# Spreading the expert gates in one pass instead of two, with half of them parked in HBM and part of the one-hot work on ScalarE

## The chip, the core and the metric

One core of a Trainium2 chip runs the whole kernel in one launch. The metric is the device time in microseconds, lower is better. Engines: TensorE (PE, with its weight loads as PEld), VectorE (DVE), ScalarE (ACT), GpSimd (POOL), and SyncE (SP), which here only issues DMAs.

## What is computed

One layer of an encoder over 512 tokens of width 1024: a mixing sublayer (Fourier, dilated attention, memory attention, gates), and then the PEER sublayer, a retrieval of single-neuron experts, which is the part that the change touches:

```python
q = (xt @ w_pq).reshape(n_tok, PEER_HEADS, 2, PEER_HALF)          # 8 heads
s1 = jnp.einsum('thc,kc->thk', q[:, :, 0], sub_keys1)             # 128 keys
s2 = jnp.einsum('thc,kc->thk', q[:, :, 1], sub_keys2)             # 128 keys
v1, i1 = lax.top_k(s1, 16); v2, i2 = lax.top_k(s2, 16)
cand = v1[..., :, None] + v2[..., None, :]
sc, ic = lax.top_k(cand, 16)                                      # 16 experts a head
e1, e2 = i1[ic // 16], i2[ic % 16]; experts = e1 * 128 + e2       # of 16384
gate = jax.nn.softmax(sc, axis=-1)
act = gelu(einsum('tkd,td->tk', u_tab[experts], x))
y = einsum('tk,tkd->td', gate * act, v_tab[experts])
h = layer_norm(ALPHA * h + y, ln2_g, ln2_b)
```

So each token sums 128 experts, each with one 4 KB row of `u_tab` and one of `v_tab`.

## The kernel before

The 512 tokens are four tiles of 128. The PEER sublayer treats them in two ways that run side by side.

**Gathered tiles (0 and 1).** There are 16 steps (8 heads, 2 tiles) of 16 experts, so 256 expert numbers per partition. For each, POOL issues an indirect DMA of 128 rows of `u_tab` (512 KB) into a ring of five (`u_row`, L604), and DVE takes the dot product with the token (`dot`, L1314). 25 places later (`LAG`) the same is done with `v_tab` (`v_row`, L613; `weigh`, L1336). One u row and one v row of this kind are called a pair; place p of the loop has the u part of expert p and the v part of expert p-25, so there are `PAIRS_IN` = 281 places. They are dealt out by hand over the stages of the program by `TAIL_PAIRS`, `TOP_PAIRS`, `REST_PAIRS`, `X_PAIRS` and `V_PAIRS`. At some places DVE also does the top-16 search of a later step (`top_halves`, `top_pairs`).

**Dense tiles (2 and 3).** These 256 tokens are multiplied with the whole tables. The tables are read in 128 pieces of 128 experts (512 KB each) through rings of three (SP, `u_table`, `v_table`). The steps are:
- S(e): PE multiplies piece e of `u_cols` with the tokens, ACT applies gelu and writes `acts[e % 64]`, which holds 64 pieces (`CW`), half of the 128.
- X: each token's 128 gates must stand at the places of its experts, over all 16384. PE makes that matrix, token by token, as a product of one-hots: key 2's one-hot against key 1's one-hot times the gate. A gate is split in a high and a low f16 part, which gives two matmuls a token. A batch b is 8 tokens (`BT`), so a pass has 32 batches. DVE makes the one-hots (`one_hots`: L1302 key 1, L1303 key 2, L1304 key 1 times both gate parts), PE multiplies (`scatter`), and DVE multiplies the result from PSUM into `acts` (`take_spread`, L1375).
- V(e): PE adds `acts[e]` times piece e of `v_tab` to `y_ps`, which stays in four PSUM banks.

`acts` has room for 64 pieces only, so everything is done in two chunks: S(0..63); X for chunk 0; V(0..63), each followed by the S of 64 pieces later; X for chunk 1; V(64..127). Every engine runs its list in program order. PE can't start X before DVE has the softmax shares of the dense tiles (`shares`), which DVE does after the 90 places that stand ahead of X. At the end DVE finishes the gathered tile's sum and norm (`gathered_norm`), waits for PE's last V, adds it to h and does the last norm.

## Time and profile before

| | us |
|---|---|
| median of 3 runs (1881.47 to 1882.58) | 1882.39 |
| the profiled execution | 1882.71 |
| its span, first to last instruction | 1880.9 |

| engine | busy us | share of the span |
|---|---|---|
| PE | 1710.1 | 91% |
| DVE | 1250.8 | 67% |
| POOL | 635.2 | 34% |
| ACT | 204.6 | 11% |

```profile
PE   7999999989999799999728899999999958799996
DVE  3343175122567669997888986777777699966664
PEclk9999999999999989999867799999999976799998
DMA  6715201954779635679992199999999991299994
```

Each character is one of 40 equal slices of the span (47 us). The digit is the busy share in tenths; PEclk is the granted TensorE clock in tenths of full speed. The two dips of the DMA row, at 1 and 2 after the first nines and at 1 and 2 near the end, are the two X passes. In this kernel all ordinary matmuls have the line L639 and all ScalarE reads of PSUM the line L887, since helpers record them, so the tiles and shapes tell the work apart.

### The profile page before, as it was taken

What the parts mean: (1) busy time and instruction counts of PE and PEld (TensorE: products, weight loads), DVE (VectorE), ACT (ScalarE), POOL (GpSimd) and SP (SyncE); (2) the same over time, 40 slices, a digit from 0 to 9 for tenths busy, and PEclk for the clock granted to TensorE, in tenths of its full rate; (3) what the DMA queues carried; (4) which work ended last, traced back from release to release, by engine and by line L of the source; (5) the groups of instructions that cost most, each with busy time, mean ns of one, the idle gap of its engine ahead of it and who ended that gap; (6) DMA issues with size and microseconds to landing.
All of it is one profiled execution on the core that took longest, in us unless ns stands there. A gap on an engine that the chain in (4) does not pass through costs nothing.

```text
span 1880.9 us, 19525 instructions
## 1 busy us (share of the span) xinstructions
PE 1710.1 (91%) x7236; PEld 1213.9 (65%) x7236; DVE 1250.8 (67%) x2616; ACT 204.6 (11%) x431; POOL 635.2 (34%) x536
## 2 busy tenths in 40 slices
PE   7999999989999799999728899999999958799996
PEld 6588878967555668888527666666666547544442
DVE  3343175122567669997888986777777699966664
ACT  1101033101111021112100000111011010000000
POOL 2000000000246200146550175765665661265340
PEclk9999999999999989999867799999999976799998
DMA  6715201954779635679992199999999991299994
GB/s 221 235 45 158 83 7 40 286 166 145 243 266 370 246 124 175 217 261 409 388 356 62 51 400 409 409 409 409 397 409 409 409 372 61 77 404 410 409 403 151
DMA packets 193834, 493.81 MB, mean 263 GB/s; under 512 B 14103, under 2 KB 92952, under 8 KB 193444
## 3 DMA queue, kind: packets, MB, share of 16 engines
q0 software_dynamic: 74672, 271.55, 37.6%
q1 hardware_dynamic: 119068, 221.01, 33.1%
q8 instruction: 58, 0.95, 0.2%
q14 instruction: 36, 0.29, 0.0%
HBM read 489.32 MB, written 7.90 MB: 264 GB/s over the span
## 4 chain that ended last, share of the span: by engine, by line
PE 43%; DVE 26%; DMA 14%; POOL 9%; issue 7%; ACT 0%; SPq 0%; DVEq 0%
PE ps L639 42%; DMA arena<-in_v_tab_dram,experts 10%; POOL arena L604 5%; DVE arena L1336 5%; POOL arena L613 4%; DVE arena L1303 2%; DVE arena L1314 2%; DMA arena<-in_v_tab_dram 2%; DVE i L1233 2%; DVE pos L1248 1%; DVE arena L1302 1%; DVE v L1232 1%; DVE best L1247 1%; PE ps L651 1%; DMA arena<-in_w_mem_kv_dram 1%
## 5 line engine op out<-in xcount | busy, mean ns | idle before, releaser
L639 PE MATMUL ps<-arena 128*128 128x256 f32 (+4 forms) x6016 | 1503.1, 412 | 75.8 <-ACT arena L887 23.1
L639 PEld LDWEIGHTS ps<-arena 128*128 128x128 f32 (+1 forms) x6016 | 1035.9, 188 | 537.9 <-issue 285.9
L604 POOL DMA_INDIRECT arena<-in_u_tab_dram,experts x256 | 326.6, 1276 | 860.5 <-DVE dots L1314 531.6
L1336 DVE SCALAR_TENSOR_TENSOR arena<-arena,coef 128x1024 f32<-128x1024 f32 x254 | 327.3, 1289 | 111.0 <-DMA arena<-in_v_tab_dram,experts 110.2
L1314 DVE CUSTOM_DVE_ANT_0 arena<-arena 128x1024 f32<-128x1024 f32 x256 | 312.4, 1224 | 87.9 <-DMA arena<-in_u_tab_dram,experts 87.7
L613 POOL DMA_INDIRECT arena<-in_v_tab_dram,experts x256 | 297.3, 1161 | 148.3 <-DVE arena L1336 97.7
L887 ACT ACTIVATE arena<-ps 128x256 f32<-128x256 f32 (+2 forms) x212 | 88.9, 427 | 765.7 <-PE ps L639 722.0
L639 PE MATMUL ps<-hotg,arena 128*128 128x64 f16 x512 | 68.1, 303 | 26.8 <-DVE hotg L1304 25.5
L639 PEld LDWEIGHTS ps<-hotg,arena 128*128 128x128 f16 x512 | 59.9, 147 | 34.7 <-DVE hotg L1304 34.7
L1198 DVE TENSOR_TENSOR arena<-arena,ps 128x128 f32<-128x128 f32 (+1 forms) x32 | 13.4, 418 | 103.0 <-PE ps L639 91.7
L887 ACT ACTIVATE arena<-ps,bT 128x128 f32<-128x128 f32 (+2 forms) x68 | 36.6, 538 | 313.5 <-PE ps L639 313.5
L1375 DVE SCALAR_TENSOR_TENSOR arena<-ps,arena 128x512 f32<-128x512 f32 x64 | 44.1, 690 | 11.8 <-PE ps L639 11.8
L639 PE MATMUL ps<-hT_low,w_high 128*128 128x512 f32 x128 | 50.0, 390 | 0.0
L639 PE MATMUL ps<-hT_high,w_low 128*128 128x512 f32 x128 | 49.8, 389 | 0.0
L639 PE MATMUL ps<-hT_high,w_high 128*128 128x512 f32 x128 | 49.8, 389 | 0.0
L651 PE MATMUL ps<-ident,arena 128*128 128x128 f32 x208 | 32.6, 314 | 17.9 <-DVE arena L1063 11.6
L597 POOL DMA_DIRECT2D arena<-in_ln_g_dram x1 | 0.6, 550 | 142.9 <-PE ps L639 142.9
L1303 DVE TENSOR_TENSOR arena<-iota_x,keyT 128x1024 f16<-128x1024 f16 x64 | 44.3, 692 | 2.2
L1136 DVE CUSTOM_DVE_ANT_0 arena<-ps,arena 128x512 f32<-128x512 f32 (+1 forms) x32 | 16.6, 556 | 39.9 <-PE ps L639 39.8
L651 PEld LDWEIGHTS ps<-ident,arena 128*128 128x128 f32 x208 | 28.5, 164 | 19.9 <-DVE arena L1063 12.8
L1195 DVE TENSOR_TENSOR arena<-arena,ps 128x128 f32<-128x128 f32 (+1 forms) x16 | 6.7, 420 | 38.0 <-PE ps L639 32.9
L651 PE MATMUL ps<-ident,keys_of 128*128 128x128 f32 x4 | 1.3, 435 | 33.0 <-DVE gate L1285 33.0
(127 smaller groups left out, 793.3 us busy)
## 6 DMA issues: line engine op xcount, KB each, us to landing
arena<-in_u_cols_dram SPq DMA_DIRECT2D x128, 512.0 KB, 6.8
arena<-in_v_tab_dram SPq DMA_DIRECT2D x128, 512.0 KB, 6.8
arena<-in_w_in_dram SPq DMA_DIRECT2D x37, 1024.0 KB, 5.6
arena<-in_w_o_dram SPq DMA_DIRECT2D x8, 1024.0 KB, 9.9
arena<-in_w_pq_dram SPq DMA_DIRECT2D x8, 1024.0 KB, 5.4
beta_copies<-beta_rows SPq DMA_DIRECT2D x1, 4608.0 KB
arena<-in_w_mem_kv_dram SPq DMA_DIRECT2D x4, 1024.0 KB, 18.6
arena<-in_w_a_dram SPq DMA_DIRECT2D x8, 512.0 KB, 6.2
```

Source lines behind the costliest of these rows:

```text
L604: nc.gpsimd.indirect_dma_start(out=u_ring[:, n % ROWS, :], out_offset=None, in_=u_tab[0], in_offset=bass.IndirectOffsetOnAxis(ap=experts[: ...
L613: nc.gpsimd.indirect_dma_start(out=v_ring[:, n % ROWS, :], out_offset=None, in_=v_tab[0], in_offset=bass.IndirectOffsetOnAxis(ap=experts[: ...
L639: return nc.tensor.matmul(dst, lhsT, rhs, start=start, stop=stop, skip_group_check=True)
L651: last = nc.tensor.transpose(bank(key, n * P, (n + 1) * P), src, ident[:])
L887: nc.scalar.activation(dst, src, func, **kw).then_inc(done, 1)
L1232: c.link(*[nc.vector.max(v12[:, x, lo:hi], half(src, x)) for x in range(2)])
L1233: c.add(*[nc.vector.max_index(i12[:, x, lo:hi], v12[:, x, lo:hi], half(src, x)) for x in range(2)])
L1247: c.link(nc.vector.max(best[:, s, lo:hi], src))
L1303: nc.vector.tensor_tensor(hot2[:, n % 2], iota_x[:], wide(keyT[:, 1, :], KEYS), ALU.is_equal)
L1314: nc.vector.tensor_tensor_reduce(row, row, h[:, GATHER[s // HEADS], :], 1.0, 0.0, ALU.mult, ALU.add, dots[:, s % 2, k:k + 1]).then_inc(u_u ...
L1336: nc.vector.scalar_tensor_tensor(out=y_acc, in0=row, scalar=by, in1=y_acc, op0=ALU.mult, op1=ALU.add).then_inc(v_used, 1)
L1375: nc.vector.scalar_tensor_tensor(out=mine, in0=bank(key).rearrange("p (e t) -> p e t", t=BT), scalar=1.0 / GATE_UP, in1=mine, op0=ALU.mult ...
```

## The change

The two X passes become one. It covers all 128 pieces at once, in 32 batches of 8 tokens. A batch still has 16 matmuls, now with 128 columns each instead of 64, and its result fills two PSUM banks, taken from banks 2 to 7 in turn. The first half is multiplied into `acts` by DVE as before. The second half is copied by ACT into `kept` (`spill`), and SP writes it to HBM (`gates_kept`, 16 writes of 512 KB). While V(0..63) and S(64..127) run, SP reads it back in eight groups of 8 pieces (`gates_in`, 1 MB each, in runs of 512 bytes), and DVE multiplies each group into `acts` (`regate`). So V(64) follows S(127) with no X between them.

The one-hots of both keys are one DVE operation of 2048 elements, DVE multiplies only the high gate part, and ACT makes the low part in eight operations of 128 elements, one a token, with the gate as a per-partition scale (`low_parts`). The places are dealt out anew: 34 instead of 42 in the last part of the S stage, 4 then 0 instead of 4 and 4 in X, 108 instead of 118 in the first V stage, and so 87 instead of 65 in the last stage. The last of the top-16 searches ahead of X moves from place 86 to place 76. The third v piece can be loaded only after X, since its ring place holds one-hots. The multiplication with ALPHA ahead of the last norm goes to ACT.

```diff
-REST_PAIRS = 42
-X_PAIRS = (4, 4)
-V_PAIRS = (118, PAIRS_IN - TAIL_PAIRS - TOP_PAIRS - REST_PAIRS - sum(X_PAIRS) - 118)
+REST_PAIRS = 34
+X_PAIRS = (4, 0)
+V_PAIRS = (108, PAIRS_IN - TAIL_PAIRS - TOP_PAIRS - REST_PAIRS - sum(X_PAIRS) - 108)
+KEPT = 2 * BT
+GRP = 8
+GATED_LAG = 4
+TOP_PAIR = {TOPK * (s - 2) + TOP_AT if s != HEADS - 1 else TOPK * (s - 2) - 4: s for s in range(2, GN)}
...
-            u.add(key, reader, bank=6 + key[2] % 2)
+            u.add(key, reader, bank=2 + 2 * (key[1] % 3), width=2)
...
-            for e in range(TAB_RING):
+            for e in range(TAB_RING - 1):
                 v_table(e)
             for e in range(TAB_RING, CW + TAB_RING):
                 u_table(e)
+            for q in range(GW // KEPT):
+                sp.wait_ge(spilled, (q + 1) * KEPT // BT)
+                sp.dma_start(gates_kept[q], kept[:, q % 2]).then_inc(gates_out[q % 2], 16)
+            wait_full(sp, ("X", BATCHES - 1))
+            v_table(TAB_RING - 1)
+            def gates_in(j):
+                if j >= 2:
+                    sp.wait_ge(regated, j - 1)
+                sp.dma_start(gates_back[j % 2].rearrange("p q e t -> p q (e t)"),
+                             gates_kept[:, :, j * GRP:(j + 1) * GRP, :].rearrange("q p e t -> p q (e t)")
+                             ).then_inc(gates_landed[j % 2], 16)
...
+                if e < 2 + TAB_RING:
+                    gates_in(e - TAB_RING)
+                elif e % GRP == GRP - 1 and 2 * GRP < e < CW + 2:
+                    gates_in(e // GRP)
...
+                pe.wait_ge(hot_ready, b + 1)
+                pe.wait_ge(low_ready, b + 1)
                 begin(key)
+                if b >= 3:
+                    pe.wait_ge(spilled, b - 2)
                 for t in range(BT):
+                    into = ps[:, units.bank[key] + t // 4, t % 4:4 * KEYS:4]
                     for i in range(2):
-                        last = mm(bank(key)[:, t:BT * CW:BT], hot2[:, n % 2, :, t], hotg[n % 2][:, i, :, t],
-                                  i == 0, i == 1)
+                        last = mm(into, hots[:, b % 2, 1, :, t], hotg[b % 2][i][:, :, t], i == 0, i == 1)
...
+            def low_parts(b):
+                if b >= 2:
+                    wait_full(sca, ("X", b - 2))
+                sca.wait_ge(hots_ready, b + 1)
+                for t in range(BT):
+                    last = nc.scalar.activation(hotg[b % 2][1][:, :, t], hots[:, b % 2, 0, :, t], ACT.Copy,
+                                                scale=low[:, b * BT + t:b * BT + t + 1])
+                last.then_inc(low_ready, 1)
+            def spill(b):
+                key, (q, i) = ("X", b), divmod(b, KEPT // BT)
+                wait_done(sca, key)
+                if q >= 2:
+                    sca.wait_ge(gates_out[q % 2], 16 * (q // 2))
...
+            low_parts(0)
+            for b in range(BATCHES):
+                if b + 1 < BATCHES:
+                    low_parts(b + 1)
+                spill(b)
...
+            def regate(j):
+                wait_done(dve, ("S", CW + (j + 1) * GRP - 1))
+                dve.wait_ge(gates_landed[j % 2], 16 * (j // 2 + 1))
+                mine = acts[:, j * GRP:(j + 1) * GRP, :].rearrange("p e (q t) -> p q e t", t=KEPT)
+                nc.vector.tensor_tensor(mine, mine, gates_back[j % 2], ALU.mult).then_inc(regated, 1)
```

How the lists of the engines change at the places that the prediction speaks of. On DVE, the first two batches of the first X pass before. `hotg` and `arena` are the two buffers of the gated one-hot, and `psum_full` is PE's signal that a product stands in PSUM:

```order
L1302 TENSOR_TENSOR arena<-iota_x,keyT 128x512 [waits h_out,dve_emptied]
L1303 TENSOR_TENSOR arena<-iota_x,keyT 128x1024 [waits dve_step]
L1304 TENSOR_TENSOR arena<-arena 128x1024
L1302 TENSOR_TENSOR arena<-iota_x,keyT 128x512 [waits hot_ready]
L1303 TENSOR_TENSOR arena<-iota_x,keyT 128x1024 [waits dve_step]
L1304 TENSOR_TENSOR hotg<-arena 128x1024
L1375 SCALAR_TENSOR_TENSOR arena<-ps,arena 128x64x8 [waits act_emptied,psum_full]
L1302 TENSOR_TENSOR arena<-iota_x,keyT 128x512 [waits hot_ready,psum_full]
```

And the same place now. L1356 makes both keys' one-hots, L1360 the high gate part, L1431 multiplies into `acts`:

```order
L1356 TENSOR_TENSOR arena<-iota_x,keyT 128x2048 [waits h_out,dve_emptied]
L1360 TENSOR_TENSOR arena<-arena 128x1024 [waits hots_ready]
L1356 TENSOR_TENSOR arena<-iota_x,keyT 128x2048
L1360 TENSOR_TENSOR hotg<-arena 128x1024 [waits hots_ready]
L1431 TENSOR_TENSOR arena<-ps,arena 128x2x64x4 [waits act_emptied,psum_full]
L1356 TENSOR_TENSOR arena<-iota_x,keyT 128x2048 [waits low_ready,psum_full]
L1360 TENSOR_TENSOR arena<-arena 128x1024 [waits hots_ready]
L1431 TENSOR_TENSOR arena<-ps,arena 128x2x64x4 [waits psum_full]
```

A batch has three DVE operations instead of four, a pass covers both chunks, and the one-hots of a batch now also wait for ACT (`low_ready`). On ACT, the list before has nothing in the X pass. Now it has, after the last gelu of S (L917), the low parts (L1014) and the copies of the second half (L1025):

```order
L917 ACTIVATE arena<-ps 128x256 [waits psum_full]
L1014 ACTIVATE arena<-arena 128x128 [waits hots_ready]
L1014 ACTIVATE arena<-arena 128x128 x7
L1014 ACTIVATE early<-arena 128x128 [waits hots_ready]
L1014 ACTIVATE early<-arena 128x128 x7
L1025 ACTIVATE arena<-ps 128x2x64x4 [waits dve_emptied]
L1014 ACTIVATE arena<-arena 128x128 [waits hots_ready,psum_full]
L1014 ACTIVATE arena<-arena 128x128 x7
L1025 ACTIVATE arena<-ps 128x2x64x4 [waits dve_emptied]
```

ACT stands between DVE and PE in every batch, and its copy of a batch waits for DVE to have taken that batch. On SP, between the last pieces of the S stage and the first of the V stage, the list now reads:

```order
L549 DMA arena<-in_v_tab_dram 128x1024 [waits psum_full]
L549 DMA arena<-in_v_tab_dram 128x1024
L544 DMA arena<-in_u_cols_dram 128x1024 [waits psum_full] x64
L565 DMA gates_kept<-arena 128x1024 [waits spilled] x16
L549 DMA arena<-in_v_tab_dram 128x1024 [waits psum_full]
L549 DMA arena<-in_v_tab_dram 128x1024 [waits vt_used,gates_out1,gates_out0]
L544 DMA arena<-in_u_cols_dram 128x1024 [waits psum_full]
L572 DMA arena<-gates_kept 128x16x128
```

The 16 writes and the first reads stand in the same list as the tables' pieces; before, the v and u pieces followed each other directly.

## Rows read from the trace of the kernel before

**Rows 1.** Busy us (and instructions) by stretch; clock, DMA share, GB/s
```profile
840.00:950.00 110.00, 95.31 (x416) 79.69 (x416) 86.82 (x155) 19.36 (x41) 72.97 (x61) 0.95 1.01 400
950.00:983.00 33.00, 0.54 (x3) 0.54 (x4) 28.91 (x61) 0.00 (x0) 19.08 (x17) 0.54 0.90 346
997.00:1076.00 79.00, 66.63 (x502) 58.42 (x499) 75.73 (x131) 0.00 (x0) 8.81 (x6) 0.68 0.16 47
1082.00:1531.00 449.00, 438.77 (x1520) 290.46 (x1519) 340.89 (x598) 46.26 (x101) 284.49 (x222) 0.99 1.02 403
1531.00:1543.00 12.00, 0.00 (x0) 0.00 (x0) 10.14 (x13) 1.20 (x1) 9.25 (x10) 0.57 1.01 394
1546.00:1634.00 88.00, 67.41 (x508) 59.18 (x506) 84.58 (x165) 1.69 (x3) 11.98 (x10) 0.67 0.21 72
1640.00:1838.00 198.00, 194.09 (x444) 81.53 (x443) 130.03 (x151) 0.65 (x3) 98.79 (x95) 1.00 1.02 401
```

**Rows 2.** Waits, longest first, of 950 to 983 us
```profile
PE ps L651 <- DVE gate L1285: 33.0, 1, 33.0
```

**Rows 3.** Timeline of the end of the kernel
```profile
1836.67 1.28 DVE L1336 SCALAR_TENSOR_TENSOR arena<-arena,coef 128x1024 f32<-128x1024 f32 x1 [1.05 <-DMA arena<-in_v_tab_dram,experts]
...
1845.02 1.28 DVE L1063 SCALAR_TENSOR_TENSOR arena<-arena,rs 128x1024 f32<-128x1024 f32 x1
...
1864.45 2.48 DVE L1412 SCALAR_TENSOR_TENSOR arena<-arena,ps 128x1024 f32<-128x1024 f32 x2 [18.14 <-PE ps L639]
```

**Rows 4.** DMA issues by line: KB each, median us to landing
```profile
arena<-in_u_cols_dram SPq DMA_DIRECT2D x128, 512.0 KB, 6.8
```

**Rows 5.** Timeline 954 to 998: start, us, engine, what [idle before, releaser]
```profile
965.41 0.48 DVE L1232 MAX8 v<-arena 128x8 f32<-128x128 f32 x2
...
973.72 1.22 DVE L1314 CUSTOM_DVE_ANT_0 arena<-arena 128x1024 f32<-128x1024 f32 x1
...
976.06 1.22 DVE L1314 CUSTOM_DVE_ANT_0 arena<-arena 128x1024 f32<-128x1024 f32 x1
...
982.46 0.69 PE L651 MATMUL ps<-ident,keys_of 128*128 128x128 f32 x2 [33.04 <-DVE gate L1285]
...
997.44 2.11 PE L639 MATMUL ps<-hotg,arena 128*128 128x64 f16 x16
997.66 0.69 DVE L1375 SCALAR_TENSOR_TENSOR arena<-ps,arena 128x512 f32<-128x512 f32 x1 [8.23 <-PE ps L639]
```

**Rows 6.** DVE, 960 to the end, by form: busy us, mean ns
```profile
L1303 DVE TENSOR_TENSOR arena<-iota_x,keyT 128x1024 f16<-128x1024 f16 x64 | 44.3, 692 | 2.2
L1375 DVE SCALAR_TENSOR_TENSOR arena<-ps,arena 128x512 f32<-128x512 f32 x64 | 44.1, 690 | 11.8 <-PE ps L639 11.8
L1302 DVE TENSOR_TENSOR arena<-iota_x,keyT 128x512 f16<-128x512 f16 x64 | 26.6, 416 | 0.2
L1304 DVE TENSOR_TENSOR hotg<-arena 128x1024 f16<-128x1024 f16 x32 | 21.9, 684 | 0.0
```

**Rows 7.** Timeline of the end of the first X pass
```profile
1071.18 2.14 PE L639 MATMUL ps<-arena 128*128 128x64 f16 x16 [0.15 <-DVE arena L1304]
...
1073.47 2.13 PE L639 MATMUL ps<-hotg,arena 128*128 128x64 f16 x16 [0.15 <-DVE hotg L1304]
1075.64 0.69 DVE L1375 SCALAR_TENSOR_TENSOR arena<-ps,arena 128x512 f32<-128x512 f32 x1 [1.59 <-PE ps L639]
1076.25 1.21 DVE L1314 CUSTOM_DVE_ANT_0 arena<-arena 128x1024 f32<-128x1024 f32 x1
1076.59 0.67 PE L639 MATMUL ps<-arena 128*128 128x512 f32 x1 [0.98 <-DVE arena L1375]
```

**Rows 8.** ACT, whole span, by form: busy us, mean ns
```profile
L887 ACT ACTIVATE arena<-ps 128x512 f32<-128x512 f32 x44 | 25.6, 593 | 45.6 <-PE ps L651 43.0 <-PE ps L639 2.6
L887 ACT ACTIVATE arena<-ps,bT 128x128 f32<-128x128 f32 x24 | 8.8, 368 | 53.3 <-PE ps L639 53.3
L887 ACT ACTIVATE arena<-ps 128x128 f32<-128x128 f32 x8 | 2.2, 278 | 12.4 <-PE ps L639 12.4
```

**Rows 9.** Stretch in which the bias is read in runs of 512 bytes
```profile
177.00:179.00 2.00, 2.00 (x11) 1.65 (x10) 0.00 (x0) 0.34 (x1) 0.00 (x0) 1.00 1.19 291
```

**Rows 10.** The page: GB/s in the 40 slices of the span
```profile
GB/s 221 235 45 158 83 7 40 286 166 145 243 266 370 246 124 175 217 261 409 388 356 62 51 400 409 409 409 409 397 409 409 409 372 61 77 404 410 409 403 151
```

More of the change, by code:

```diff
@@ L181, in dense_units @@
             out += [(("ET", r), "dve") for r in range(GT)]
+    out += [(("X", b), "dve") for b in range(BATCHES)]
     for c in range(CHUNKS):
-        out += [(("X", c, b), "dve") for b in range(BATCHES)]
         for i in range(CW):
@@ L238, in plan @@
         u.add(key, reader)
-    u.before["y"] = {u.owner[b] for b in range(2, 6)} - {None}
     for key, reader in dense_units():
@@ L409, in build @@
         keyT = sb("keyT", [P, 2, GW], F16)
-        gateT = at(168, 2).bitcast(F16)[:, 0:2 * GW].rearrange("p (i t) -> p i t", i=2)
+        gateT = at(168, 2).bitcast(F16)[:, 0:GW]
         scaled = early[:, 256:512].rearrange("p (i t) -> p i t", i=2)
-        hotg_1 = sb("hotg_1", [P, 2, CW, BT], F16)
-        hotg = [hotg_0, hotg_1[:]]
+        hotg_1 = sb("hotg_1", [P, KEYS, BT], F16)
+        hotg = [[vt_ring[:, TAB_RING - 1, i * 512:(i + 1) * 512].bitcast(F16).rearrange("p (e t) -> p e t", t=BT)
+                 for i in range(2)],
+                [hotg_1[:], early[:, 768:1280].bitcast(F16).rearrange("p (e t) -> p e t", t=BT)]]
+        low = at(168, 2)[:, GW:2 * GW]
         ps = ctx.enter_context(nc.psum_tensor("ps", [P, BANKS, 512], F32))
@@ L868, in _ @@
                         tail_unit(("ET", r))
+            for b in range(BATCHES):
+                scatter(b)
             for c in range(CHUNKS):
-                for b in range(BATCHES):
-                    scatter(c, b)
-                if c == 0:
-                    for key in sorted(units.before["y"], key=lambda k: units.index[k]):
-                        wait_done(pe, key)
                 for i in range(CW):
@@ L1007, in _ @@
                 after_pairs(v_pairs(c, CW - ACT_LAG), v_pairs(c, CW))
+            sca.wait_ge(h_in, 16)
+            nc.scalar.activation(h_back, h_back, ACT.Copy, scale=ALPHA).then_inc(h_scaled, 1)
         @block.vector
```

114 lines of the change are left out of this document (63 added, 51 removed).

## Prediction

> **What bounds the kernel now.** I read the busy times by stretch first. From 1082 to 1531 (V(0..63) with S(64..127)) PE is busy 439 of 449 us, but the DMA engines are full as well: 403 GB/s at a share of 1.02, and in the next 12 us, when PE has nothing left, 394 GB/s go on flowing, since the gathered pairs of that stage are late [rows 1]. The last stage is the same, 401 GB/s until 1838. The two X passes are the opposite: 47 and 72 GB/s, DVE busy 76 of 79 and 85 of 88 us, ACT and the DMA engines nearly idle [rows 1]. Ahead of the first X pass PE stands idle for 33 us, because DVE has not done its 90 places and the shares [rows 2], while the DMA engines still move 346 GB/s [rows 1]. So three things follow each other: DMA, then DVE in X, then DMA, then DVE again, then DMA, and PE's last V ends it: DVE waits 18 us for it and then needs 16.45 us to the end (1864.45 to 1880.9) [rows 3]. Everything from the V stage on is priced below in bytes, not in PE time.
>
> **Part 1, ahead of X.** Eight places fewer stand before the shares: 16 rows of 128 x 4 KB, each the size of a table piece (512 KB, 0.524 MB [rows 4]), 8.4 MB, at the 400 GB/s of 840 to 950 [rows 1] 21 us; DVE alone would give 8 x 2.4 = 19 us (976.06 less 973.72 is 2.34 for one place [rows 5]). I take 20. The search that moves from place 86 to 76 takes 8.3 us (965.41 to 973.72 [rows 5]). It now falls where rows are late, so they pile up behind it and the places after it run at DVE's pace: between 0 and 8 us, I take 4. The shares come at 982.5 - 24 = 958.5. PE then needs 15 us for three transposes a tile and S(61..63), as before (982.46 to 997.44 [rows 5]): 973.5. What is new: ACT must make the low parts of batch 0, and its list has the gelu of S(63) ahead of them, which ends after PE's last S. Before, DVE had the one-hots ready and waited 8 us for PE [rows 5]. That adds 0.4 + 2.5 us: X(0) starts at 976.5 instead of 997.4.
>
> **Part 2, one X batch.** Durations: the one-hots of 2048 elements, from 416 ns for 512 and 692 for 1024 [rows 6], so 0.54 ns an element and 140 fixed: 1.25 us; the high part 0.68; the take 0.69 (the same 512 elements) [rows 6]. DVE: 2.6 us a batch and 32 batches, against 64 batches of 2.3 (1073.47 less 1071.18 is 2.29 [rows 7]). ACT: one copy of 128 elements is 278 ns, and with a per-partition operand 368 [rows 8]; the trace shows no ACT operation f16 to f16 with a stride, so bounds are 8 x 0.22 and 8 x 0.40 us, 1.8 to 3.2. I take 2.45, the 368 row with a little overlap between neighbours. The spill copy is 0.59 [rows 8]. ACT: 3.05 a batch. PE: 16 matmuls start to end in 2.14 [rows 7], so 0.12 us each and 0.18 at the end, with 64 columns. With 128 columns the spacing is between the same (the weight loads, which are 128 columns as before, set it) and twice that (the moving columns set it): 2.15 to 4.05 us a batch. The clock level doesn't settle it, for the granted clock is 0.68 in that pass, a mix of 1.2 and 2.4 GHz [rows 1]. I take 2.3, near the first, since in the V and S stage PE is busy 439 of 449 us with 290 us of weight loads beneath it [rows 1]: they are hidden there, and so one of the two sets the pace, not their sum.
>
> The Trainium skill (ScalarE: Activation LUTs, What ACT_TABLE_LOAD costs) says that each pointer operand adds about 93 ns and that neighbouring activations overlap by about 93. The rows agree with the first (368 against 278). By that page eight of them would be an estimated 2.4 us, which would leave the sum as it is.
>
> No engine's sum sets the period, though, but the loop. Two batches are in flight (the buffers of the one-hots are two), and DVE's list has the take of b right before the one-hots of b+2. So two periods hold one-hots, low parts, the 16 matmuls, take, and four handovers of some 0.06: 1.25 + 2.45 + 2.3 + 0.69 + 0.23 = 6.9 us, a period of 3.46. The lower bound is ACT's own 3.0, the upper (3.2 and 4.05 put in) 4.7. The four places in X cost some 2 us each, as the other engines go on meanwhile. From X(0) to the first V: 31 x 3.46 + 3 x 2 + the last batch with matmuls, take and spill 3.7 = 117 us. V(0) starts at 976.5 + 117 = 1093.5, where before it was 1076.6 [rows 7]. So the single pass takes 38 us more than the first one did (79.2) and the second, with its wait, goes: 1531 to 1634, 103 us. The writes to HBM (8.4 MB in 117 us) find the DMA engines idle; SP's list behind them has only pieces that wait for X anyway.
>
> **Part 3, from V(0) on.** Count what must still land. Places 86 to 280 take 195 v rows and 170 u rows, less the ten that stand in the rings: 355. Tables: 126 pieces of v and 61 of u: 187. Together 542 x 0.524 = 284.2 MB, at 403 GB/s [rows 1] 705 us. The same count for the first V stage of before (118 places and 125 pieces, 189 MB) against 403 x 449 + 394 x 12 = 185.7 MB moved from 1082 to 1543 is 2% too high, so this way of counting stands. New: the gates come back, 8.4 MB in runs of 512 bytes. The bias is read in such runs at 291 GB/s with the engines full [rows 9], so 29 us and not 21. Reading h back is 3 us. Sum 737 us. Bounds: 409 GB/s, as in the full slices of the page [rows 10], gives 11 less; 395 gives 14 more.
>
> PE needs in this time 449 us [rows 1] and then the 230 of its last stage before (1634 to DVE's wake-up at 1864.45 [rows 1, 3]), 679 us in all. That is less than 737, so for the first time the end isn't PE's: the pairs are last. The moved work is visible here: before, the last stage held 65 places, now 87, and 22 places more are 44 rows, 23 MB, 57 us of DMA that partly stood in the S, V and X stages before. What was late before (V(127)) ends 60 us earlier than the pairs. Regating (8 x 2048 elements, 8 x 2.2 us by 4 x the 512 of L1375) and the searches lie beside: DVE is busy 341 of 449 us there [rows 1], and ten rows in the rings are 20 us of cover. If DVE were late by more than 20 us at one spot, the rest would show.
>
> Start-up of the stage 5.4 us (V(0) at 1076.6, full from 1082), last rows at DVE's and POOL's pace 2, then the last v row and the gathered norm (1836.67 to 1846.3: 9.6 us) and the final 16.45 [rows 3]. End: 1093.5 + 5.4 + 737 + 2 + 9.6 + 16.45 = 1864. Against 1880.9 that is 17 less. Outside the span lie 1.8 us (1882.71 less 1880.9), and the profiled execution is 0.3 above the median: 1865.5. ALPHA on ACT costs and gains nothing: h is there long before, and DVE's operation is still the same one.
>
> [...]
>
> **Rivals.**
> A. The X period is long, and the change loses. If the columns (or their stride) set the spacing of 0.12 us in the rows, a batch needs 4.05 on PE, two periods hold 8.65, the period is 4.33: 27 us more, 1892. It decides from a period of 4.0 on (31 x 0.54 = 17 us eat the gain). For: 64 columns at 1.2 GHz are 53 ns and weight loads 107, so the row can't tell which; the same 2.1 us stand at both clock levels. Against: nothing in S and V suggests it.
> B. The loop doesn't bind, ACT's 3.0 us a batch does, because the low parts are shorter or overlap with the tail of the matmuls. 14 us less than forecast: 1851. For: 278 ns is the shorter of the two rows. With 409 GB/s in the long stage it is 1841.
> C. The gates' return costs double (runs at a bad pitch, or fights with the gathers): 29 us more, 1894. For: the only price for such runs is one short read. Against: at 512 bytes it still moved 291 GB/s.
> D. The change doesn't do what it says: the early shares don't come, since the stage ahead is held by the tables of S and not by the pairs, and PE's idle time stays: 24 us given back, 1889. Against: PE's idle 33 us waits for DVE alone [rows 2].
> E. The V/S stage stalls: ACT's gelus wait in order behind the pairs, the pairs get less of the DMA, PE waits. PE has 60 us to spare, so up to that it costs nothing, and the forecast stays.
>
> **How the numbers follow.** Forecast with E: 0.45. B: 0.20. A: 0.17. C: 0.07. D: 0.05; other things that end close to before 0.06. About 0.2% (3.8 us) is what a measurement can tell from no change. Faster takes B, nearly all of the forecast's own range (1850 to 1880) and little of the others: 0.65. Slower takes A, C, D: 0.27. Same: 0.08. The predicted time is 1865. The range takes in B with the fast DMA at the low end, and A and C at the high: 1838 to 1895.
>
> **What would show it.** Right: X from about 976 to 1093 in one pass at 3.4 to 3.5 us a batch, with DVE waiting for PE in each; 400 to 409 GB/s without a break from 1100 until about 1835; DVE's last weigh after PE's last V by some 60 us; PE's idle time ahead of the transposes down from 33 to some 9 us. Wrong: a period of 4 us or more in X, 16 matmuls over 3 us, the DMA share under 1 in the last stage with DVE or POOL never waiting for rows, or a chain that ends on PE.

## The result, and the profile after

| | before | changed | ratio (95% interval) |
|---|---|---|---|
| median of 4 runs, us | 1882.08 | 1965.12 (1961.35 to 1971.02) | 1.0444 (1.0416 to 1.0472) |
| profiled span, us | 1880.9 | 1961.6 | |
| X(0) / V(0) start, us | 997.4 / 1076.6 | 967.9 / 1149.0 | |
| last matmul ends, us | 1864.4 | 1888.5 | |
| start of V(0) to start of the last v row's weigh, us | 760 | 787 | |

The change made the kernel 4.4% slower; 1865 us was forecast, and 1965 lies far outside the range of 1838 to 1895. The changed kernel's page, in 40 slices of 49 us, with ACT's busy share, the granted clock and GB/s, and two of its DMA issues (KB each, us from issue to landing):

```profile
ACT  1101042111120121121399930000001001000000
PEclk9999999999999899999666676998999899999975
GB/s 212 226 65 139 75 2 126 267 145 172 246 328 350 146 138 202 232 410 408 231 69 65 65 223 397 315 407 378 373 365 409 379 394 282 402 409 409 409 372 169
...
arena<-gates_kept SPq DMA_DIRECT2D x8, 1024.0 KB, 25.9
gates_kept<-arena SPq DMA_DIRECT2D x16, 512.0 KB, 2.6
```

Two stretches are wrong at sight. Counted from 0, slices 20 to 22 lie wholly in the X pass: ACT, which was to be one engine among several, stands at 9 there. And from slice 24 on, where 403 GB/s were to flow without a break (what full slices look like is in [rows 10]), 315, 378, 373, 365, 379 and 282 stand between slices of 394 to 409.

The same in busy time by stretch; columns are length, then PE, PEld, DVE, ACT and POOL with their instructions, the granted clock, the DMA share and GB/s. The rows answer [rows 1]: the first the idle stretch ahead of X, the second the X passes, the third a part of the stage of V:

```profile
925.00:949.00 24.00, 7.63 (x36) 6.38 (x34) 22.59 (x52) 1.15 (x3) 15.50 (x13) 0.74 1.01 394
967.00:1149.00 182.00, 124.79 (x513) 71.83 (x513) 84.61 (x102) 166.24 (x282) 8.07 (x6) 0.62 0.16 61
1217.00:1329.00 112.00, 112.00 (x386) 73.63 (x386) 70.85 (x108) 9.23 (x22) 59.65 (x46) 0.99 0.95 367
```

ACT is busy 166 of the 182 us in X. DVE, which bound both X passes before (76 of 79 and 85 of 88 us), is busy for less than half of the time. In this part of the V stage DVE (71 of 112 us) and POOL (60) are far from full and the DMA share is still under 1: the DMA engines are short of requests, not of time.

One batch and a half of X in order of time (start, length, engine, line; in brackets the idle time before it and what ended it), where a batch of half the width took 2.29 us before [rows 7]:

```profile
989.41 0.92 ACT L1025 ACTIVATE arena<-ps 128x512 f32<-128x512 f32 x1
989.87 0.69 DVE L1360 TENSOR_TENSOR hotg<-arena 128x1024 f16<-128x1024 f16 x1
989.99 3.91 PE L667 MATMUL ps<-arena 128*128 128x128 f16 x16 [2.02 <-issue]
990.23 4.93 ACT L1014 ACTIVATE early<-arena 128x128 f16<-128x128 f16 x8
993.94 0.69 DVE L1431 TENSOR_TENSOR arena<-ps,arena 128x512 f32<-128x512 f32 x1 [3.38 <-PE ps L667]
994.54 1.22 DVE L1356 TENSOR_TENSOR arena<-iota_x,keyT 128x2048 f16<-128x2048 f16 x1
...
995.85 4.94 ACT L1014 ACTIVATE arena<-arena 128x128 f16<-128x128 f16 x8 [0.27 <-DVE arena L1356]
```

Eight low parts take 4.93 us where 2.45 was taken, the spill copy 0.92 where 0.59 was, and both follow each other with almost no gap: ACT's list sets a period of 5.6 us (990.23 to 995.85). The 16 matmuls take 3.91 us, near the upper bound of 4.05. DVE's one-hots of 2048 elements, 1.22 us, and its high part, 0.69, are as forecast. The groups by form say the same (count, busy us, mean ns of one, idle time before):

```profile
L1014 ACT ACTIVATE early<-arena 128x128 f16<-128x128 f16 x128 | 79.0, 1051 | 9.6 <-DVE arena L1356 9.6
L1025 ACT ACTIVATE arena<-ps 128x512 f32<-128x512 f32 x32 | 28.9, 902 | 4.5 <-DVE arena L1431 4.3
```

1.05 us for one low part (about 0.55 from the start of one to the next, as they overlap) stands against the 368 ns of the row from which it was priced [rows 8]. The other buffer's group reads alike (1053 ns).

The waits say what was late. First PE ahead of the transposes, which answers [rows 2], then three large waits between 1149 and 1657 (sum, count, longest):

```profile
PE ps L679 <- DVE gate L1342: 16.9, 1, 16.9
...
PE ps L667 <- DMA arena<-in_v_tab_dram: 51.2, 6, 16.3
DVE coef L1378 <- ACT act L991: 51.2, 6, 24.2
DVE arena L1439 <- DMA arena<-gates_kept: 43.1, 3, 15.8
```

The early shares came: they are at 949.4 us (the end of L1342) against 958.5 forecast. PE's waiting of 33.0 us is 16.9 and not the 9 of the forecast, since PE had finished its pieces earlier too (at 932.6, before at 949.4). But the V stage has waits that before did not have: PE for pieces of v's table, DVE for the gates, DVE for ACT's gelus. The end of the kernel, which answers [rows 3]:

```profile
1934.24 2.67 DVE L1392 SCALAR_TENSOR_TENSOR arena<-arena,coef 128x1024 f32<-128x1024 f32 x2 [1.10 <-DMA arena<-in_v_tab_dram,experts]
```

DVE ends on the last v row (a DMA), whose weigh starts at 1935.6 and ends at 1936.9, and no longer on PE's last V, which was done at 1888.5. This part of the forecast holds. So the miss is 55 us up to V(0) (1149.0 against 1093.5) and 42 us after it (787 against 744 to the start of the last weigh). The experiments take them one at a time.

### The profile page after: what moved, and what is told of

It is laid out like the page before. It is cut to its first block, busy times and chain, and to the rows that moved or that the text cites. A ratio compares the mean times of both kernels' runs of the same rounds, so it can differ in the third digit from the quotient of the medians.

```text
span 1961.6 us, 18701 instructions
## 1 busy us (share of the span) xinstructions
PE 1705.4 (87%) x6724; PEld 1163.4 (59%) x6724; DVE 1198.9 (61%) x2464; ACT 376.3 (19%) x720; POOL 646.2 (33%) x536
## 4 chain that ended last, share of the span: by engine, by line
PE 55%; DMA 19%; DVE 14%; issue 7%; POOL 5%; ACT 0%; SPq 0%; DVEq 0%; ACTq 0%; POOLq 0%
PE ps L667 54%; DMA arena<-in_v_tab_dram 7%; DMA arena<-in_u_tab_dram,experts 5%; DMA arena<-in_v_tab_dram,experts 4%; POOL arena L641 3%; POOL arena L632 2%; DVE arena L1392 2%; DVE i L1290 1%; DMA arena<-in_w_in_dram 1%; DVE pos L1305 1%; DMA arena<-in_w_mem_kv_dram 1%; DVE arena L1370 1%; DVE v L1289 1%; DVE best L1304 1%; PE ps L679 1%
## 5 line engine op out<-in xcount | busy, mean ns | idle before, releaser
L667 PE MATMUL ps<-arena 128*128 128x256 f32 (+5 forms) x5760 | 1506.5, 423 | 115.9 <-DMA arena<-in_v_tab_dram 56.5
L667 PEld LDWEIGHTS ps<-arena 128*128 128x128 f32 (+2 forms) x5760 | 1011.7, 190 | 605.4 <-issue 306.3
L917 ACT ACTIVATE arena<-ps 128x256 f32<-128x256 f32 (+2 forms) x212 | 88.8, 428 | 763.7 <-PE ps L667 721.9
L917 ACT ACTIVATE arena<-ps,bT 128x128 f32<-128x128 f32 (+2 forms) x68 | 36.6, 538 | 313.1 <-PE ps L667 313.1
L1431 DVE TENSOR_TENSOR arena<-ps,arena 128x512 f32<-128x512 f32 x32 | 22.1, 692 | 106.6 <-PE ps L667 106.6
L1014 ACT ACTIVATE early<-arena 128x128 f16<-128x128 f16 x128 | 79.0, 1051 | 9.6 <-DVE arena L1356 9.6
L667 PE MATMUL ps<-hotg,arena 128*128 128x128 f16 x128 | 52.9, 413 | 31.8 <-issue 31.8
L1014 ACT ACTIVATE arena<-arena 128x128 f16<-128x128 f16 x128 | 78.9, 1053 | 1.6 <-DVE arena L1356 1.6
L1255 DVE TENSOR_TENSOR arena<-arena,ps 128x128 f32<-128x128 f32 (+1 forms) x32 | 13.4, 418 | 104.4 <-PE ps L667 90.9
L1439 DVE TENSOR_TENSOR arena<-arena 128x2048 f32<-128x2048 f32 x8 | 18.4, 2295 | 81.8 <-DMA arena<-gates_kept 43.1
L667 PE MATMUL ps<-early,arena 128*128 128x128 f16 (+1 forms) x160 | 60.0, 406 | 0.8 <-issue 0.8
L667 PEld LDWEIGHTS ps<-hotg,arena 128*128 128x128 f16 x128 | 18.5, 145 | 48.4 <-issue 39.2
## 6 DMA issues: line engine op xcount, KB each, us to landing
arena<-gates_kept SPq DMA_DIRECT2D x8, 1024.0 KB, 25.9
```

The lines of the kernel that those rows point to most:

```text
L667: return nc.tensor.matmul(dst, lhsT, rhs, start=start, stop=stop, skip_group_check=True)
L917: nc.scalar.activation(dst, src, func, **kw).then_inc(done, 1)
L1014: last = nc.scalar.activation(hotg[b % 2][1][:, :, t], hots[:, b % 2, 0, :, t], ACT.Copy, scale=low[:, b * BT + t:b * BT + t + 1])
L1431: nc.vector.tensor_tensor(mine, ps[:, bk:bk + 2, 0:4 * CW].rearrange("p k (e t) -> p k e t", t=4), mine, ALU.mult).then_inc(done, 1)
```

## The experiments

Medians are in us; the ratio is to the kernel before, whose runs beside these had medians of 1881.2 to 1881.3. Theory L: the miss before V(0) is the length of ACT's low part. Its rival is the forecast's rival A, that PE's matmuls set the X period. Theory G: the miss after V(0) is the gates' read in 512-byte packets. Its rivals are that the X pass alone pushes everything back, and that the pairs and the gelus stall each other (E).

**e1: the low part on DVE.** One more operation of 1024 elements there, none on ACT. The low gate parts that it reads are kept in f16, where ACT's scale had them in f32. In short form:

```
+ nc.vector.tensor_tensor(hotg[b % 2][1], hots[:, b % 2, 0], low[:, toks]..., ALU.mult)
- for t in range(BT): nc.scalar.activation(hotg[b % 2][1][:, :, t], ..., ACT.Copy, scale=low[...])
```

> The changed kernel, but the low gate part is made by VectorE again, in one more operation of 1024 elements (0.68 us a batch), and ScalarE has only the copies of the second half. Theory (ScalarE's eight strided operations, 4.9 us a batch, set the period of X at 5.67 us): the period falls to what the 16 matmuls need, 3.9 to 4.1 us, X takes 125 to 133 us instead of 181, and the whole falls by 45 to 55 us, to about 1915. Rival (the loop of waits or the wider matmuls set the period, whoever makes the low part): the period stays above 5 us and the whole moves by less than 20 us.

Measured: 1904.21, ratio 1.0123 (1.0093 to 1.0152), 61 us less than the changed kernel. The period is 3.93 us (first to 32nd take: 971.1 to 1093.1), V(0) starts at 1094.5. Of e1's trace between 940 and 1200, the matmuls of one batch and the groups of the spill copy and the take:

```profile
1029.01 3.91 PE L667 MATMUL ps<-arena 128*128 128x128 f16 x16
...
L1024 ACT ACTIVATE arena<-ps 128x512 f32<-128x512 f32 x32 | 19.2, 600 | 107.4 <-DVE arena L1427 107.4
L1427 DVE TENSOR_TENSOR arena<-ps,arena 128x512 f32<-128x512 f32 x32 | 22.1, 691 | 29.2 <-PE ps L667 29.2
```

So both are true, one above the other: ACT set 5.67 us, and with ACT out of it PE's 16 matmuls of 3.9 us set 3.93. DVE waits for PE 29.2 us in 32 takes. The spill copy is 600 ns again. That the strided operations ahead of it on ACT had made it longer, and not just any operation close ahead, is shown by e4 below: right behind operations with a stepped output it takes 917 to 927 ns, right behind those with the output in a row 573 to 597.

**e2: the gates in long runs.** HBM holds them by group, so that the read has 8 KB a partition; the 16 writes have the short runs in its place:

```
- gates_kept = nc.dram_tensor("gates_kept", [GW // KEPT, P, CW, KEPT], F32)
+ gates_kept = nc.dram_tensor("gates_kept", [CW // GRP, P, GW // KEPT, GRP * KEPT], F32)
```

> The changed kernel, but the gates lie in HBM so that a group is read back in runs of 8 KB a partition; the short runs of 512 bytes are on the writes in X, when the DMA engines are idle. Bytes and order are the same. Theory (a read of 2048 packets of 512 bytes takes its turns packet by packet against the gathers' 4 KB packets, 26 us for 1 MB, and SP's table pieces stand behind it in the same queue): a group lands in 8 to 12 us, PE's waits for v pieces in the V and S stage fall from 51 us to under 10, and the whole falls by 25 to 45 us, to about 1930. Rival (the stage is late only because of the bytes, gates and 22 more places): the waits stay and the whole moves by less than 10 us.

Measured: 1920.71, ratio 1.0222 (1.0192 to 1.0253), 44 us less, with the X period unchanged (5.66). The issue row of the reads and PE's wait for v pieces over the whole kernel:

```profile
arena<-gates_kept SPq DMA_DIRECT2D x8, 1024.0 KB, 10.9
...
PE ps L668 <- DMA arena<-in_v_tab_dram: 5.3, 8, 1.0
```

A read lands in 10.9 us instead of 25.9, and PE waits 5.3 us for pieces instead of 56.5 over the whole kernel. DVE's waits for the gates and for L991's gelu (43.1 and 51.2 us before the edit) are gone from the V stage. From V(0) to the start of the last weigh it is 740 us instead of 787. The writes in X, now in short runs, cost nothing to be seen (3.2 us to land against 2.6, the same period).

**e3: both.**

> Both edits together. Theory: the two costs are in different stages and add, 70 to 95 us less than the changed kernel, 1870 to 1895, so about as fast as before the change. Rival (what one gives back the other loses, since the last stage is bound by DMA bytes anyway): no more than the larger of the two alone, 1910 or so.

Measured: 1862.01, ratio 0.9907 (0.9879 to 0.9935). The two effects add (61 and 44 us alone, 103 together), so neither hid behind the other. By stretch:

```profile
968.00:1091.00 123.00, 116.26 (x496) 71.45 (x494) 102.14 (x132) 19.01 (x32) 8.06 (x6) 0.96 0.31 90
1091.00:1540.00 449.00, 448.74 (x1551) 295.85 (x1552) 330.02 (x550) 46.22 (x99) 239.04 (x208) 1.00 1.02 406
1540.00:1765.00 225.00, 219.23 (x498) 91.41 (x496) 159.45 (x241) 6.79 (x12) 143.73 (x115) 1.00 1.03 407
1765.00:1834.00 69.00, 0.00 (x0) 0.00 (x0) 56.38 (x59) 2.13 (x2) 45.83 (x36) 0.52 0.90 323
```

This is nearly the picture that the forecast drew: 406 and 407 GB/s with a share of over 1 until PE is through, 68 us before the last weigh. Only in those last 69 us the rate is 323 GB/s and not over 400. With the two mis-sized terms taken out, V(0) comes at 1091.3 (forecast 1093.5), the last weigh starts at 1832.7 (forecast 1838), and the time is 1862 (forecast 1865). That V(0) agrees is luck: X starts at 964.1, 12 us ahead of the forecast, and takes 127 us, 10 more, with another mix of work in a batch. The agreement of the long stage is better founded: 399 GB/s over 742 us are 296 MB, and the forecast's count is 294 with the gates and h. Its time (741 us against 744) still holds two offsetting errors, the slow last stretch (an estimate of 14 us by 22.3 MB at 403 GB/s) and prices for short gates runs, start-up and last rows that this kernel pays only in part.

**e4: what makes an operation long.** Batches 2f and 2f+1 modulo 12 use one of six forms (f as in `f = b // 2 % 6`), of ACT's and of PE's operands. The gates land in wrong places, so this kernel doesn't compute the layer and serves for durations alone. ACT's forms, in short form:

```
+ toc = hotg[..][1].rearrange("p e t -> p (e t)")[:, t * KEYS:(t + 1) * KEYS]   # 128 in a row
+ if f == 0: activation(to, fr, ..., scale=by)     # as in the changed kernel, 16-byte step
+ elif f == 1: activation(to, frc, ...)            # input in a row
+ elif f == 2: activation(toc, fr, ...)            # output in a row
+ elif f == 3: activation(toc, frc, ...)           # both
+ elif f == 4: activation(to, fr, ..., scale=0.5)
+ else: activation(toc, frc, ..., scale=0.5)
```

> The changed kernel, in which the batches of X use six forms of the same operations in turn, each form for a whole batch (the gates come out in wrong places, so the output is not the reference's). ScalarE: as is; input contiguous; output contiguous; both; as is with an immediate scale; both contiguous with an immediate scale. PE: as is; moving operand contiguous; output contiguous; stationary operand contiguous; 64 columns; all contiguous. Theory (strided f16 costs ScalarE 1.05 us for 128 elements where 0.37 was expected, and the moving operand's stride of 16 bytes costs PE 0.234 us a matmul of 128 columns): with both sides contiguous the ScalarE operation takes 0.3 to 0.4 us and the scale's kind only 0.09 of it; the matmul with a contiguous moving operand falls to about 0.12. Rival (f16, or the per-partition scale, makes the operation slow; and the 128 columns at 1.2 GHz plus the weight load make the matmul): the ScalarE operation stays at 1.0 whatever the stride, or falls only with the immediate scale, and the matmul stays at 0.2 or more with all operands contiguous.

Measured: one run of 1937.81, of which only the durations count. ACT by line, with the shortest, median and longest of one in ns; the lines are the forms in their order, the fifth (as is, with an immediate factor, 1064 ns) left out:

```profile
L1035 ACT ACTIVATE early<-arena x24: 866/1086/1106, 967.0 to 1087.9; 128x128 f16<-128x128 f16 x24
L1037 ACT ACTIVATE early<-arena x24: 865/1072/1110, 978.7 to 1098.7; 128x128 f16<-128x128 f16 x24
L1039 ACT ACTIVATE early<-arena x24: 501/507/534, 989.0 to 1108.1; 128x128 f16<-128x128 f16 x24
L1041 ACT ACTIVATE early<-arena x24: 386/386/403, 998.4 to 1116.6; 128x128 f16<-128x128 f16 x24
...
L1045 ACT ACTIVATE early<-arena x16: 292/292/309, 1018.0 to 1077.8; 128x128 f16<-128x128 f16 x16
```

It is the step of the output: 1086 ns with it and 507 without, while the input's alone changes nothing (1072). With both in a row it is 386, near the 368 of [rows 8], and the per-partition factor is 94 ns of that (292 without it). In spacing from one start to the next the four are 570, 415, 292 and 199 ns (as is, output in a row, both, both with an immediate). PE's forms are told apart by the spacing from one matmul to the next, and it has to be read at one level of the granted clock at a time, since X has stretches at both:

| PE form, ns from start to start (median) | 2.4 GHz granted | 1.2 GHz granted |
|---|---|---|
| as is | 234 (from e1) | 233 |
| moving operand in a row | 109 | 213 |
| output in a row | 232 | 233 |
| weights in a row | 228 | 227 |
| as is, 64 columns | 120 | 122 |
| all three in a row | 56 | 107 |

A batch with the moving operand in a row at 2.4 GHz here, and one at 1.2 GHz from e10 below (each with a row of its stretch for PE alone: length, busy time, granted clock, DMA share, GB/s):

```profile
1036.28 1.94 PE L887 MATMUL ps<-arena 128*128 128x128 f16 x16 [1.72 <-issue]
1036.00:1038.30 2.30, 1.94 (x16) 1.00 0.38 151
...
1013.43 3.63 PE L671 MATMUL ps<-arena 128*128 128x128 f16 x16 [7.32 <-DVE arena L1361]
1013.00:1017.10 4.10, 3.63 (x16) 0.51 0.38 115
```

The moving operand's step is what rival A had put in brackets: with it a matmul takes 233 ns at either level, and at 16 x 0.233 + 0.18 it makes the 3.9 us. It goes with the columns (122 for 64 of them), so the 0.12 us of [rows 7] were set by the stepped columns too. Without it the clock decides, and at 1.2 GHz only 20 ns are gained as long as the weights and the output keep their steps. Which of these two holds the 109 and 213 above the 56 and 107 of the last form wasn't separated.

**e5: the short runs kept, but on their own queue.** The gates are read from ACT's list, not from SP's, so the table pieces no longer stand behind them:

```
- sp.dma_start(gates_back[j % 2]..., gates_kept[:, :, j * GRP:(j + 1) * GRP, :]...)
+ nc.scalar.dma_start(gates_back[j % 2]..., gates_kept[:, :, j * GRP:(j + 1) * GRP, :]...)
```

> The changed kernel with its layout of short runs, but the eight reads of the gates are issued by ScalarE, at the same places of the stage, so they have a hardware queue of their own and the table pieces don't stand behind them. Theory (the harm is the place in SP's queue, not the DMA time of short packets, which is 3.6 to 4.1 us a group): PE's waits for v pieces in the V and S stage fall from 51 us to under 10 although a group still takes 20 us or more to land, and the whole falls by 25 to 45 us, as with long runs. Rival (short packets slow the 16 engines down for everybody): a group's landing and PE's waits stay, and the whole moves by less than 10 us.

Measured: 1925.53, ratio 1.0245 (1.0217 to 1.0272), 40 us less than the changed kernel: nearly all of what e2 gives, with the same packets. The queue's row, PE's wait over the whole kernel and the stage:

```profile
arena<-gates_kept ACTq DMA_DIRECT2D x8, 1024.0 KB, 40.1
...
PE ps L656 <- DMA arena<-in_v_tab_dram: 6.5, 9, 1.4
...
1149.00:1660.00 511.00, 502.17 (x1672) 318.82 (x1672) 374.18 (x625) 49.68 (x104) 280.23 (x234) 0.99 1.03 399
```

A read now takes even longer, 40.1 us, and does no harm: PE waits 6.5 us for pieces, and the stage moves 399 GB/s. DVE's waits for the gates and for L991 are gone here as well. So most of the loss was not what the read takes of the DMA engines (rival C of the forecast) but what stands behind it in SP's queue.

**e6: 16 more places in X.** `X_PAIRS = (4, 0)` becomes `(20, 0)` in the changed kernel, as the DMA engines stand idle there.

> The changed kernel with 20 instead of 4 places in X and 71 instead of 87 in the last stage. Theory (VectorE stands idle for 107 us in X, since ScalarE sets the period, and the time from V(0) on is bytes by DMA rate): the period of X hardly grows (0 to 15 us over the pass), 16 places are 32 rows or 16.8 MB less from V(0) on, 42 us at 403 GB/s, and the whole falls by 25 to 42 us. Rival (VectorE's work in X sits on the loop of waits, 2.4 us a place): X grows by 38 us and the whole stays within 10 us.

Measured: 1912.78, ratio 1.016 (1.014 to 1.018), 52 us less, more than the upper end expected. The pass from first to last take is 19 us longer (period 6.28). From V(0) to the last weigh it is 716 us against 787, 71 less, where the 32 rows of 0.524 MB are only 42 us at 400 GB/s. PE's wait for v pieces is 42.5 us over the whole kernel against 56.5; how the remaining gain splits over the stalls wasn't taken apart.

**e7: e3 with 20 places in X.**

> Low part on VectorE, long runs, and 20 places in X. Here X is bound by the matmuls at about 3.85 us a batch, with VectorE idle for 28 us of the pass. Theory: of 39 us of added work in X some 15 to 25 show, 42 us go from V(0) on, so 15 to 27 us less than the version with both edits (1862): 1835 to 1847. Rival (the last stage is by now bound by PE, as before the change): no gain, 1860 or more.

Measured: 1841.82, ratio 0.9793 (0.9775 to 0.9812), the fastest of all.

```profile
967.00:1118.00 151.00, 119.57 (x498) 70.47 (x496) 137.66 (x181) 21.79 (x36) 49.61 (x37) 0.75 0.57 178
1122.00:1570.00 448.00, 448.00 (x1555) 294.96 (x1553) 335.49 (x578) 45.87 (x98) 244.90 (x206) 1.00 1.02 408
```

V(0) comes 28 us later than in e3, 1.8 for a place, since DVE is now busy 138 of the 151 us of X, which moves 178 GB/s instead of 90. Each place moved there takes two rows of 0.524 MB, 2.6 us at 403 GB/s, out of the stage that is bound by DMA. Measured, V(0) to the last weigh falls by 46 us (741 to 695), 2.9 a place.

**e8: the low part stays on ACT, but is written in token rows** (on top of e2); PE reads it so, and both steps of that operand are gone:

```
- nc.scalar.activation(hotg[b % 2][1][:, :, t], ...)
+ nc.scalar.activation(by_token(hotg[b % 2][1])[:, t, :], ...)    # p e t stored as p (t e)
```

> The changed kernel with long runs, and the low part still on ScalarE, but written token by token in a row of 128 elements (PE reads it so), so that ScalarE's output and half of PE's moving operands are contiguous. Theory (the stride of the output is what makes ScalarE's operation 1.05 us, that of the moving operand what makes 0.234 us a matmul): ScalarE's operation falls to 0.51 with 0.42 between starts, 8 of them 3.4 us, the 16 matmuls to 2.9 us, the period to 4.0 to 4.4, X to 130 to 145 us, and the whole to 1870 to 1885. Rival (with spill and low parts in one list the waits bind): the period stays at 5 us or more, and the whole near the 1921 of long runs alone.

Measured: 1887.24, ratio 1.003 (1.0014 to 1.0045), period 4.63. ACT between 940 and 1120:

```profile
L1019 ACT ACTIVATE early<-arena 128x128 f16<-128x128 f16 x128 | 54.8, 515 | 12.9 <-DVE arena L1361 12.9
```

1051 ns became 515, as e4 said. The change's plan, low parts on ACT, then costs 5.67 - 4.63 = 1.04 us a batch less, but is still 0.7 us a batch longer than DVE's way (3.93). The period is above the 4.0 to 4.4 expected and the time just outside. Part of this is the clock: a pair of matmuls (one moving operand with the step, one without) takes 0.32 us where 2.4 GHz is granted and 0.43 at 1.2, and 16 of them take 2.8 us in the five batches wholly at 2.4 GHz, but 3.2 in the median of those with both levels, where 2.9 was expected. By the forecast's own loop an estimate is (1.22 + 3.42 + 3.2 + 0.69 + 0.23) / 2 = 4.4 us: the low parts stand in the chain before the matmuls. The remaining 0.25 us stays open.

**e9 and e10: DVE writes token rows**, the low part alone (e9) and both parts (e10), on top of e7, so that PE's spacing falls. In short form:

```
- nc.vector.tensor_tensor(hotg[b % 2][i], hots[:, b % 2, 0], ..., ALU.mult)
+ nc.vector.tensor_tensor(by_token(hotg[b % 2][i]).rearrange("p t e -> p e t"), hots[:, b % 2, 0], ..., ALU.mult)
```

> The version with low part on VectorE, long runs and 20 places, but VectorE writes the low part token by token in rows of 128 elements (its output then has a stride), and PE reads that half of its moving operands without a stride. Theory (X is bound by the moving operand's stride): the matmul after it falls from 0.234 to 0.11 to 0.12 us, 16 of them from 3.75 to 2.9 us, and if VectorE's operation grows only from 0.68 to 1.2 us, X falls by 10 to 20 us and the whole to 1822 to 1832. Rival (VectorE pays for a strided f16 output as ScalarE did, 5 ns an element): the operation takes 5 us, X grows by 100 us, the whole is over 1920.

> The same, with both gate parts written token by token. Theory: 16 matmuls take 2.0 us, VectorE is the bound of X at 1.2 + 2 x 1.2 + 0.7 = 4.3 us a batch, so X is no faster than in the version with one part in rows, or some 10 us slower: 1825 to 1845. Rival: as for the one part, twice: over 2000.

Measured: 1947.74, ratio 1.0361 (1.0336 to 1.0387), and 2076.28, ratio 1.1036 (1.101 to 1.1062). DVE of e9, the low part with the step and the high part without:

```profile
L1361 DVE TENSOR_TENSOR early<-arena 128x1024 f16<-128x1024 f16 x16 | 75.2, 4703 | 0.0
L1359 DVE TENSOR_TENSOR hotg<-arena 128x1024 f16<-128x1024 f16 x16 | 11.1, 692 | 0.5
```

The same 1024 elements take 4703 ns in place of 692 when neighbours in the operation's order lie 256 bytes apart, so DVE loses 4 us a batch for each part. PE saves next to nothing: with both parts in rows its 16 matmuls were expected at 2.0 us and take 3.63 (the e10 row above), with 1.2 GHz granted throughout in 25 of 31 batches. PE stands idle between them, 7.32 us ahead of that row.

## Why the prediction was wrong

**The failed step of Part 2: "I take 2.45, the 368 row with a little overlap".** The low part's output has a step of 16 bytes between its elements; the 368 row had none. The spacing is 570 ns (the median in e4) instead of 306, and eight are 4.93 us. The bounds of 1.8 to 3.2 were not bounds: both came from rows of operands without a step, while the text itself said that no row shows a stride. e1, e4 and e8 show it from three sides (taken away: -61 us; output in a row: 507 ns; on ACT in token rows: 515 ns and period 4.63). With a length like this, the loop of two batches isn't what binds (with the measured lengths it gives (1.22 + 4.93 + 3.9 + 0.69 + 0.23) / 2 = 5.5 us), ACT's own list is: 4.93 + 0.9 = 5.8 us of busy time, with some overlap a period of 5.67. Times 31 it is 176 us, where the forecast had 107.

The Trainium skill (SBUF — State Buffer, Door 1: The DMA port swizzle) notes that SBUF is organised in 16-byte cachelines, and that every access that crosses to a new line pays. By that, a step of 16 bytes makes each f16 element a line of its own, where in a row eight share one. The trace agrees in kind for ACT's output, for DVE's output (4703 against 692) and for PE's moving operand (234 against 109 at 2.4 GHz), but not for ACT's input as long as the output has the step (1086 against 1072). PE's weights in a row gain little beside a stepped moving operand (227 against 233), and what they would gain without it wasn't measured alone.

**PE's 16 matmuls, taken at 2.3, are 3.9 us.** The bounds (2.15 to 4.05) held them. The wrong choice was to take the weight loads for what sets the 0.12 us of the rows, by the V and S stage. It was the moving columns with their step (e4: 122 ns for 64 of them, 233 for 128). Rival A had the place, the price (4.05) and even the word stride, but its period added ACT's 2.45; e1, with no low parts on ACT, gives 3.93. In the changed kernel itself A didn't decide anything, for ACT's list was longer still.

**The early shares, Part 1, came 9 us earlier than forecast** (949.4 against 958.5), so rival D is out, and X(0) was at 967.9 against 976.5. The gain of 33 us was forecast as 24, 20 for the places and 4 for the search. Even with all of the search's 8.3 us the sum would be 28 to 29, so the rest has another cause, which stays open. That hid 9 us of the miss: 64 us came from the X pass itself (181 us against 117).

**Part 3, the failed step: "29 us and not 21" for the gates.** They were priced as time of the DMA engines alone, and as that they were right: the 2048 packets of a read take 59 us of engine time, 3.7 for each of the 16 engines, 29 in eight reads. What failed is that nothing was charged for what stands behind them: the queue was not walked, though the order list ahead of the forecast shows the reads among the tables' pieces. A gates read at 1329.01 and what follows it, in the changed kernel:

```profile
1329.01 0.43 SPq L572 DMA_DIRECT2D arena<-gates_kept  x1
1332.07 9.65 SPq L549 DMA_DIRECT2D arena<-in_v_tab_dram  x1
...
1356.22 2.29 DVE L1439 TENSOR_TENSOR arena<-arena 128x2048 f32<-128x2048 f32 x1 [14.35 <-DMA arena<-gates_kept]
1357.44 1.22 PE L667 MATMUL ps<-arena 128*128 128x512 f32 x1 [8.17 <-DMA arena<-in_v_tab_dram]
```

The read is 2048 packets of 512 bytes. By the records of the packets they run from 1334.7 to 1355.6, and in these 20.9 us the engines also moved 1733 packets of 4 KB, 1600 of them of POOL's gathers: a turn of SP's queue yields an eighth of the bytes of a turn of POOL's. A small packet takes 27 ns of an engine's time and one of the gathers 168 (medians), so an estimate for 128 such turns on each of the 16 engines is 25 us, near the 25.9 of a read's landing. The piece of v behind the read comes only 25 us after its issue, PE waits 8.17 us for it and DVE 14.35 for the gates.

How this reaches the pairs is to be seen where the first two reads (issued at 1159 and 1174) have passed:

```profile
1216.60 45.71 PE L667 MATMUL ps<-arena 128*128 128x512 f32 x150 [16.32 <-DMA arena<-in_v_tab_dram]
1225.40 0.38 ACT L917 ACTIVATE arena<-ps 128x256 f32<-128x256 f32 x1 [24.64 <-PE ps L667]
1239.77 0.23 DVE L1378 SCALAR_TENSOR_TENSOR coef<-gate,gate_inv,act 128x16 f32<-128x16 f32 x1 [24.22 <-ACT act L991]
```

PE got its piece 16.32 us late. So ACT's gelus of the S stage came late, the gelu of the pairs (L991) stands behind three of them in ACT's list, and DVE waited 24.22 us for that. Until DVE goes on, the rings of the pairs don't come free and nothing new is gathered: in the window of 1217 to 1329 the DMA falls to 367 GB/s though no gates are read in it (300 GB/s until 1240, 408 from 1262 on). The waits, 51.2 us for the gelus and 43.1 for the gates, sum to more than twice the 42 us that were lost, so part of them was made up again; that the loss came through them is shown by e2 and e5, where neither is left. e5 shows that the place in the queue matters and not the bytes: same packets, a slower landing, 40 us less.

The Trainium skill (DMA: Bandwidth & Descriptors, Queues, rings and completion order) says that an engine goes round-robin between queue rows and drains a whole packet, there a group of descriptors, from one before it switches. The trace agrees that the queues share the turns and not the bytes, 2048 small packets against 1733 of 4 KB in one window; how many records of the profile make one turn it doesn't show.

**Rival C** (the gates at twice the cost) named the place but not the mechanism. The bad pitch that it allows for is not seen: the runs of one partition lie 512 KiB apart in HBM, and a packet takes 27 ns of an engine's time (36 at most in 95 of 100), no more than the bias' 512-byte runs of [rows 9] (34). **Rival E** had the mechanism, and its price ("PE has 60 us to spare, so up to that it costs nothing") was wrong: a stall of PE passes on through ACT's and DVE's ordered lists to the pairs, which are the bound.

**What was right:** the DMA bound of the long stage and its byte count (e3: 406 and 407 GB/s until PE is through, 296 MB against 294), the pairs and not PE as the end, and the fixed tail behind it (26.0 us from the start of the last weigh, 26.05 forecast). The chance for slower, 0.27, lay on A, C and D; none of them reached 1965, because no case held two failures together, nor an ACT operation three times its row.

## What to carry to other kernels

Price an operation by its access pattern, not by its element count: where no row has the same step in the output or in the moving operand, the row without a step is a lower end, not a bound on both sides. When a transfer is added, walk the queue that it joins as well as its bytes: short packets in a shared in-order queue hold back everything behind them, and another queue or a layout with long runs (the short ones put in the write, where the DMA engines are idle) takes that away. When one stage is bound by DMA and another by an engine, count how many us of DMA a place moved into the idle stage saves (2.6 by its bytes here, 2.9 measured) against what it adds there (1.8 here). When two forms of a matmul are compared, compare them at the same granted clock: a median over both levels had promised 2.0 us for 16 matmuls that took 3.63.

## What the runs showed of the hardware

- ScalarE, 128 f16 elements: 1086 ns with a 16-byte step of the output, 507 with the output in a row, 386 with both in a row, 292 with an immediate factor too. A copy from PSUM close behind operations with a stepped output takes 902 to 927 ns instead of 600 (changed kernel, e4).
- VectorE, 1024 f16 elements: 692 ns, or 4703 where the output steps by 256 bytes (e9).
- TensorE, 128 columns f16, from start to start: 233 ns with a 16-byte step of the moving operand at either level of the granted clock; without it 109 at 2.4 GHz and 213 at 1.2; with all operands in a row 56 and 107 (e4). Beside a stepped moving operand, the output or the weights in a row changed little (232 and 228).
- A read of 1 MB in 512-byte packets beside 4 KB gathers landed in 25.9 us in SP's queue and 40.1 in ACT's (e5), against 10.9 with 8 KB runs (e2); its packets took 3.7 us of each DMA engine.
- One core sustained 406 to 408 GB/s over 450 us (e3, e7).
